# A two-layer streaming encoder: forget gate in quarter tiles, queries' norm weights applied after the turn back, last outputs turned by channel, two splits and four waits moved

## The chip, the cores and the metric

The kernel runs on one core of a Trainium2 chip. The core has five engines with instruction streams of their own: TensorE (PE), VectorE (DVE), ScalarE (ACT), GpSimd (POOL) and SyncE (SP, which only issues DMAs here). They meet through semaphores. The metric is the device time of one launch in microseconds (us), the median of several runs.

## The reference

One step of an encoder with two layers, on 256 new frames behind 16 meta tokens and 32 frames of a running stream, 304 columns in all (`T`); the model's width is 2048.

```python
# layer 0: mLSTM, 8 heads of 512, INNER = 4096
xm, z = split(rmsnorm(x, norm_g) @ w_in)           # 2048 -> 2 x 4096
xc = silu(causal_conv(xm, buf, conv_w, conv_b))
q, k = einsum(xc, wq), einsum(xc, wk) * 512 ** -0.5   # per head
v = einsum(xm, wv)
ig, lf = gates of (q, k, v) @ w_gate                # lf = log_sigmoid
h, (C, n, m) = mlstm_run(q, k, v, ig, lf, state)    # decayed scores, old state C0 enters with a * (q @ C0)
y = ((layernorm(h) * out_g + skip * xc) * silu(z)) @ w_out;  x = x + y
# shared keys, values and forget stream
kvf = rmsnorm(x, kv_norm_g) @ w_kvf                 # 2048 -> 2048 + 2048 + 16
k = rmsnorm(kvf[..., :2048] by head, k_norm_g);  v = kvf[..., 2048:4096]
logf = log_sigmoid(kvf[..., 4096:] + b_f)           # the forget gate, 16 heads
# layer 1: attention with forgetting, 16 heads of 128
q, z = split(rmsnorm(x, norm_g) @ w_in);  q = rmsnorm(q by head, q_norm_g)
s = q @ k.T * 128 ** -0.5 + cumsum(logf)[query] - cumsum(logf)[key], causal
x = x + ((softmax(s) @ v) * silu(z)) @ w_out
```

Returned are the outputs of both streams and all keys, values, forget values and states.

## The kernel before

**Chunks.** Every large weight comes in chunks of 512 rows by 256 columns, 400 in all. A chunk goes through four steps, each on its own engine and each with four buffers: SP loads it (`load_chunk`, `raw`, L146), ACT rounds it to `w_hi` (`high_part`, L152), DVE makes the rest `w_lo` (`low_part`, L157), and PE multiplies (`products`, L177 to L179): for two output tiles `m` and four row tiles `k` it adds w_hi·x_hi, w_hi·x_lo and w_lo·x_hi, 24 matmuls in fp32r, into the PSUM tiles `acc`. SP loads chunk n once DVE has split chunk n - 4; ACT and DVE split n + 2 while they belong to chunk n.

**Slots.** The order of every engine is written by hand: one loop over chunks, and beside each chunk small events with a letter. All engines walk through the same tables (`FIRST_NEXT`, `BESIDE_OUT`, `END_OUT`, `BESIDE`), each with its own function for a letter; an event that comes early in a slot delays the split behind it on ACT and DVE. In the tables of the first layer `O` is PE's outputs of a head, and for ACT and DVE the split of the old sums (`high_old`, `low_old`); `D` are the denominators' sums. In the second layer `q` turns the queries to tokens, `r` and `n` make their norms, `f` the final queries, `b` turns them back, `X` are scores, `y` the outputs' turn.

**Stages.** x is turned to channels and scaled beside the first eight chunks (`START`, `BESIDE0`); then come the eight heads' projections, 14 chunks each (`turn`, with the score products and transposes of the head before in `post`); the last head's turn (`last_z`, `last_qkv`) also makes the gates; then eight rounds of recurrence beside the z and out projections (`state_turns`); 64 chunks of keys and values (`kv_*`, four groups of 16), of which the first group also has the norm (`norm_1`, `columns`) and the forget gate (`extras` on PE, `forget_1` to `forget_3`); and 96 chunks of the second layer (`fox_*`).

**The forget gate before.** `wf` is 128 columns wide per row tile: 16 columns w_hi, at 32 another 16 w_lo, the rest zero. Per row tile two matmuls, against x_hi and x_lo, 32 in all, fill `aux[3]`; DVE adds the two strips, scales with rstd and adds the bias.

**The queries before.** `q_finals` multiplies each of 12 pieces of 128x128 by its norm (a column) and by `gq`, the norm weights repeated on all partitions by one DMA; PE then turns the pieces back (`q_back`) and DVE copies them out of PSUM.

**The end.** `turn_y(c)` turns four channel tiles of x to three PSUM banks, one per block of tokens, once all four tiles have been summed; ACT and DVE copy the banks out, SP stores them.

## Time and profile before

| | us |
|---|---|
| median of 3 runs (lowest, highest) | 1683.02 (1681.72, 1683.88) |
| the profiled execution: time, span | 1681.52, 1679.7 |
| PE busy, PE weight loads busy | 1655.9, 1587.4 |
| DVE, ACT, POOL busy | 1075.7, 804.8, 301.8 |
| HBM read, written | 260.5 MB, 46.8 MB |

The span is the time in which the engines work; launch and end lie outside. The granted clock of PE was 1.00 over the span. The page cuts the span in 40 slices of 42 us: PE is at 9 tenths in all but the first and the last, DVE between 4 and 8, ACT between 3 and 5. PE's busy time is that of modelled ends, so the start times of its matmuls are the safer measure.

### The profile page before, as it was taken

To read this page: it belongs to the slowest core of one execution; us is meant where nothing else is said; L and a number is where in the kernel's file an instruction comes from. 1 tells how busy PE (TensorE), PEld (TensorE's weight loads), DVE (VectorE), ACT (ScalarE), POOL (GpSimd) and SP (SyncE) were. 2 spreads that over 40 slices of the span, in tenths; PEclk is the share of its full clock that TensorE was granted. 3 is DMA by queue.
4 is the path that set the end of the run, shared out by engine and by line. 5 is a ranking of instruction groups with operands and counts; after the bars stand their busy time and mean duration, and the time that the engine had idled before them with its cause. 6 is when DMAs were issued, how large, how long until landed. Compare 5 with 4: busy or idle time off the path is not lost.

```text
span 1679.7 us, 29485 instructions
## 1 busy us (share of the span) xinstructions
PE 1655.9 (99%) x11873; PEld 1587.4 (95%) x11873; DVE 1075.7 (64%) x2074; ACT 804.8 (48%) x1339; POOL 301.8 (18%) x580
## 2 busy tenths in 40 slices
PE   8999999999999999999999999999999999999998
PEld 6999999999988999999999989999999998999998
DVE  5966655655558868768687788665535645563755
ACT  5545344544554534445344445554443555535443
POOL 1202220122143332222322222021112000000000
PEclk9999999999999999999999999999999999999999
DMA  6546554655586676666766655365558554555533
GB/s 189 168 138 218 168 181 137 207 179 179 154 264 187 204 240 183 224 190 199 240 183 224 190 180 176 114 217 187 184 190 285 179 163 150 168 182 164 155 113 108
DMA packets 244344, 309.26 MB, mean 184 GB/s; under 512 B 14056, under 2 KB 219648, under 8 KB 244208
## 3 DMA queue, kind: packets, MB, share of 16 engines
q1 hardware_dynamic: 214352, 215.32, 42.1%
q0 software_dynamic: 29200, 91.23, 15.7%
q8 instruction: 94, 1.54, 0.4%
q10 hardware_dynamic: 656, 0.82, 0.2%
q14 instruction: 42, 0.34, 0.1%
HBM read 260.53 MB, written 46.79 MB: 183 GB/s over the span
## 4 chain that ended last, share of the span: by engine, by line
PE 88%; DVE 6%; ACT 3%; issue 1%; DMA 1%; ACTq 0%; POOL 0%; DVEq 0%
PE acc L177 24%; PE acc L178 24%; PE acc L179 24%; PE aux L1460 3%; PE aux L1302 2%; DVE w_lo L157 2%; PE aux L1433 1%; PE aux L1307 1%; ACT w_hi L152 1%; PE aux L1280 1%; PE aux L2710 1%; PE aux L1467 1%; PE aux L1479 1%; PE aux L2117 1%; DVE q_t L2523 1%
## 5 line engine op out<-in xcount | busy, mean ns | idle before, releaser
L157 DVE TENSOR_TENSOR w_lo<-raw,w_hi 128x1024 fp32r<-128x1024 f32 x400 | 485.7, 1221 | 371.6 <-ACT w_hi L152 369.9
L177 PE MATMUL acc<-xg_hi,w_hi 128*128 128x304 f32 x1536 | 472.8, 308 | 2.9 <-issue 1.6
L152 ACT ACTIVATE w_hi<-raw 128x1024 fp32r<-128x1024 f32 x400 | 413.9, 1055 | 104.8 <-PE acc L179 78.5
L179 PE MATMUL acc<-xg_hi,w_lo 128*128 128x304 f32 x1536 | 463.9, 302 | 0.0
L178 PE MATMUL acc<-xg_lo,w_hi 128*128 128x304 f32 x1536 | 463.0, 301 | 0.0
L177 PEld LDWEIGHTS acc<-xg_hi,w_hi 128*128 128x128 f32 x1536 | 289.6, 189 | 5.7 <-issue 1.8
L178 PEld LDWEIGHTS acc<-xg_lo,w_hi 128*128 128x128 f32 x1536 | 290.5, 189 | 0.9
L179 PEld LDWEIGHTS acc<-xg_hi,w_lo 128*128 128x128 f32 x1536 | 289.8, 189 | 0.0
L104 POOL TENSOR_TENSOR cell<-cell 1x1 f32<-1x1 f32 x159 | 73.7, 463 | 1107.8 <-DVE xc_lo L875 320.1
L177 PE MATMUL acc<-xb_hi,w_hi 128*128 128x288 f32 x512 | 156.3, 305 | 0.9 <-DVE w_lo L157 0.9
L177 PE MATMUL acc<-hz_hi,w_hi 128*128 128x304 f32 x512 | 155.3, 303 | 0.4 <-DVE zs L938 0.4
L178 PE MATMUL acc<-hz_lo,w_hi 128*128 128x304 f32 x512 | 155.1, 303 | 0.0
L179 PE MATMUL acc<-hz_hi,w_lo 128*128 128x304 f32 x512 | 154.3, 301 | 0.0
L179 PE MATMUL acc<-xb_hi,w_lo 128*128 128x288 f32 x512 | 151.9, 297 | 0.0
L178 PE MATMUL acc<-xb_lo,w_hi 128*128 128x288 f32 x512 | 151.7, 296 | 0.0
L177 PEld LDWEIGHTS acc<-xb_hi,w_hi 128*128 128x128 f32 x512 | 96.6, 189 | 2.0 <-DVE w_lo L157 1.6
L177 PEld LDWEIGHTS acc<-hz_hi,w_hi 128*128 128x128 f32 x512 | 96.4, 188 | 1.2 <-DVE hz_lo L1188 0.8
L178 PEld LDWEIGHTS acc<-xb_lo,w_hi 128*128 128x128 f32 x512 | 96.5, 188 | 0.4
L179 PEld LDWEIGHTS acc<-hz_hi,w_lo 128*128 128x128 f32 x512 | 96.7, 189 | 0.0
L178 PEld LDWEIGHTS acc<-hz_lo,w_hi 128*128 128x128 f32 x512 | 96.2, 188 | 0.3
L179 PEld LDWEIGHTS acc<-xb_hi,w_lo 128*128 128x128 f32 x512 | 96.1, 188 | 0.0
L730 ACT ACTIVATE C_out<-aux 128x512 f32<-128x512 f32 x32 | 19.2, 599 | 131.7 <-PE aux L1460 130.0
(499 smaller groups left out, 3000.9 us busy)
## 6 DMA issues: line engine op xcount, KB each, us to landing
raw<-in_a_w_in SPq DMA_DIRECT2D x128, 512.0 KB, 4.0
raw<-in_a_w_out SPq DMA_DIRECT2D x64, 512.0 KB, 4.3
raw<-in_w_kvf SPq DMA_DIRECT2D x64, 512.0 KB, 4.8
raw<-in_b_w_in SPq DMA_DIRECT2D x64, 512.0 KB, 4.6
raw<-in_b_w_out SPq DMA_DIRECT2D x32, 512.0 KB, 3.5
raw<-in_a_wq SPq DMA_DIRECT2D x16, 512.0 KB, 3.8
raw<-in_a_wk SPq DMA_DIRECT2D x16, 512.0 KB, 3.6
raw<-in_a_wv SPq DMA_DIRECT2D x16, 512.0 KB, 5.0
```

What stands on the lines that cost most here:

```text
L104: own.done(own.eng.tensor_tensor(cell, cell, cell, ALU.mult))
L152: act.activation(w_hi[:, s, :, :], raw[:, s, :, :], ACT.Copy).then_inc(hi_made, 1)
L157: dve.tensor_tensor(w_lo[:, s, :, :], raw[:, s, :, :], w_hi[:, s, :, :].bitcast(F32), ALU.subtract).then_inc(lo_made, 1)
L177: pe.matmul(acc[b][:, 0:width], wh, x_hi[:, k0 + k, :], start=st, stop=False)
L178: pe.matmul(acc[b][:, 0:width], wh, x_lo[:, k0 + k, :], start=False, stop=False)
L179: mm = pe.matmul(acc[b][:, 0:width], wl, x_hi[:, k0 + k, :], start=False, stop=last and k == 3)
L730: act.activation(C_out[:, d % 2, :], aux[u.turn(3)][:, :], ACT.Copy).then_inc(b_free[u.turn(3)], 1)
L1280: mm = pe.matmul(gate_sum[r:r + 32, 0:T], wg_in[:, HT * g + d, :], (q_T, k_T, v_T)[g][:, d, :], start=h.a == 0 and g == 0, stop=h.a == LAS ...
L1302: mm = pe.matmul(aux[b][0:n, c:c + T - t0], k_T[:, d, t0:t0 + n], q_T[:, d, t0:T], start=d == 0, stop=d == HT - 1)
L1307: mm = pe.transpose(aux[b][0:n, d * P:(d + 1) * P], (k_T, v_T)[(k - 2) // 3][:, d, t0:t0 + n], ident[:, :])
L1433: mm = pe.matmul(aux[b][:, :], p_, v_, start=k == 0, stop=t < 2 and k == len(parts) - 1)
L1460: mm = pe.matmul(aux[b][:, :], k_, v_, start=k == 0, stop=k == len(parts) - 1)
```

## The change

Eight edits:

1. `START`: ACT splits chunk 0 before it scales x columns 0 to 3; DVE splits it after column 0 and not after column 1; PE goes through chunk 0 by `k` and not by `m`. The squares of x (`squares`) go from chunks 2, 3, 3 to chunks 0, 2, 3.
2. `tokens_taken` of the last head's turn stands ahead of chunk 1 and not of chunk 0.
3. `take_pairs` is cut in two: after the last head the first copy stands ahead of `gates_whole`, the others behind it.
4. Letter `L` takes over the split of the old sums; for head 0 it stands one slot before `O` and ahead of `D`. Elsewhere it stands where `O` did. `set_old_fold` moves to `E`.
5. Forget gate: `wf` becomes 32 columns of fp32, scaled by `kv_norm_g` on DVE; 16 matmuls against x itself go to four quarter tiles (32 columns of PE each, `tile_position`), and one more matmul with `f_fold` adds the four quarters. The steps around it move by one or more chunks.
6. Queries: `q_finals` multiplies by the norm alone, three instructions of 128x512; the norm weights are a column per head (`gq`, 128x4, four DMAs) and come in when `q_back` copies out of PSUM.
7. `selections` leave `q_terms` for a slot of their own, `s`.
8. `turn_y` goes by channel tile and writes the three banks in turn; each tile's sum is waited for by itself.

```diff
-        def products(pe, n, tile, x_hi, x_lo, k0, first, last, ready=None):
+        def products(pe, n, tile, x_hi, x_lo, k0, first, last, ready=None, by_k=False):
...
+            steps = [(m, k) for k in range(4) for m in range(2)] if by_k else [(m, k) for m in range(2) for k in range(4)]
...
-        FIRST_NEXT = {0: "E P Q", 1: "D", 2: "O Z", 3: "N M", 4: "K", 5: "T0 T1", 6: "T2 T3 S0 S1 H0 H1",
+        FIRST_NEXT = {0: "E P Q", 1: "L D", 2: "O Z", 3: "N M", 4: "K", 5: "T0 T1", 6: "T2 T3 S0 S1 H0 H1",
...
+            high_part(act, Count(0))
             act.wait_ge(par_taken, 1)
-            high_x(range(0, 2))
-            high_part(act, Count(0))
-            high_x(range(2, 4))
+            high_x(range(0, 4))
             high_part(act, Count(1))
...
-                for t in {2: (0,), 3: (1, 2)}.get(n, ()):
+                for t in {0: (0,), 2: (1,), 3: (2,)}.get(n, ()):
                     squares(t)
...
-            parts_of(range(0, 2))
+            take_x(0)
+            take_x(1)
+            low_x(0)
             low_part(dve, Count(0))
+            low_x(1)
             parts_of(range(2, 4))
...
                 if j == 4:
+                    take_pairs(Count(LAST))
                     gates_whole()
-                    take_pairs(Count(LAST))
+                    take_more_pairs(Count(LAST))
...
-                if j == 0:
+
+                if j == 1:
                     tokens_taken(Count(LAST - 1))
...
-        wf = sb("wf", [P, KD, P], F32R, p3)
+
+        wf = sb("wf", [P, KD, 32], F32, p3)
+        f_all, f_fold = sb("f_all", [P, T], F32, p3), sb("f_fold", [P, BH], F32, p3)
...
+            def forget_0():
+                dve.wait_ge(f_done, 1)
+                dve.tensor_copy(f_all[:, :], aux[3][:, 0:T]).then_inc(f_out, 1)
...
-                if j == 9:
+                if j == 10:
                     pe.wait_ge(cols_taken, 1)
-                    pe.wait_ge(f_lo, 1)
+                    pe.wait_ge(f_scaled, 1)
+
                     for k in range(KD):
-                        for part, x in enumerate((xk_hi, xk_lo)):
-                            mm = pe.matmul(aux[3][:, 0:T], wf[:, k, :], x[:, k, :], start=k == 0 and part == 0,
-                                           stop=k == KD - 1 and part == 1)
+                        r = 32 * (k % 4)
+                        mm = pe.matmul(aux[3][r:r + 32, 0:T], wf[:, k, :], xT[:, k, :], start=k < 4, stop=k >= KD - 4,
+                                       skip_group_check=True, tile_position=(0, r))
                     mm.then_inc(f_done, 1)
                 if j == 11:
+                    pe.wait_ge(f_out, 1)
+                    pe.matmul(aux[3][0:BH, 0:T], f_fold[:, :], f_all[:, :], start=True, stop=True).then_inc(f_done, 1)
+                if j == 12:
                     pe.wait_ge(f_dve, 1)
...
-        QUERIES = {0: "q", 1: "r n K0 K1", 2: "f K2 K3", 4: "b"}
...
+        QUERIES = {0: "q", 1: "r n K0 K1", 2: "f K2 K3", 3: "s", 4: "b"}
...
-                pool.dma_start(gq[:, :], src.unsqueeze(0).to_broadcast([P, HD])).then_inc(gq_landed, 16)
+                for m in range(GRP):
+                    pool.dma_start(gq[:, m:m + 1], src[m * P:(m + 1) * P].rearrange("(p a) -> p a", a=1))\
+                        .then_inc(gq_landed, 16)
...
-                dve.wait_ge(gq_landed, 16 * (g + 1))
                 for t in range(3):
-                    for m in range(GRP):
-                        d = slice(m * P, (m + 1) * P)
-                        k = GRP * t + m
-                        ins = dve.scalar_tensor_tensor(q_t[:, t, d], q_t[:, t, d], qst[:, 3, k:k + 1], gq[:, d],
-                                                       ALU.mult, ALU.mult)
-                    ins.then_inc(q_final, 1)
+                    y = qst[:, 3, GRP * t:GRP * (t + 1)].unsqueeze(2).to_broadcast([P, GRP, P])
+                    dve.tensor_tensor(head_parts(q_t[:, t, :], P), head_parts(q_t[:, t, :], P), y, ALU.mult)\
+                       .then_inc(q_final, 1)
 
             def q_back(g):
+
+                dve.wait_ge(gq_landed, 16 * GRP * (g + 1))
...
-                for u in range(tile, tile + 4):
+                banks = [free_bank(use(LAST_G, f"y{c}", t)) for t in range(3)]
+                for k in range(4):
+                    u = tile + k
                     pe.wait_ge(acc_free[u % 4], u // 4 + 1)
-                for t, (t0, _) in enumerate(QT):
-                    bank = free_bank(use(LAST_G, f"y{c}", t))
-                    for k in range(4):
+                    for bank, (t0, _) in zip(banks, QT):
                         mm = pe.transpose(bank[:, k * P:(k + 1) * P], xT[:, 4 * c + k, META + t0:META + t0 + P],
                                           ident[:, :])
```

How the instructions stand. ACT beside the first chunks, before, from the first scaling on: `xg_hi` are scaled x columns, `w_hi` splits of a chunk, `sq_junk` squares of x.

```order
L580 ACTIVATE xg_hi<-xT,par 128x304 x2
L152 ACTIVATE w_hi<-raw 128x1024
L580 ACTIVATE xg_hi<-xT,par 128x304 x2
L152 ACTIVATE w_hi<-raw 128x1024
L580 ACTIVATE xg_hi<-xT,par 128x304 x2
L152 ACTIVATE w_hi<-raw 128x1024
L580 ACTIVATE xg_hi<-xT,par 128x304 x3
L152 ACTIVATE w_hi<-raw 128x1024 x2
L580 ACTIVATE xg_hi<-xT,par 128x304 x3
L590 ACTIVATE sq_junk,small<-x_tok 128x2048
```

The same stretch now:

```order
L152 ACTIVATE w_hi<-raw 128x1024
L580 ACTIVATE xg_hi<-xT,par 128x304 x4
L152 ACTIVATE w_hi<-raw 128x1024
L580 ACTIVATE xg_hi<-xT,par 128x304 x2
L152 ACTIVATE w_hi<-raw 128x1024
L590 ACTIVATE sq_junk,small<-x_tok 128x2048
L580 ACTIVATE xg_hi<-xT,par 128x304 x3
L152 ACTIVATE w_hi<-raw 128x1024 x2
L580 ACTIVATE xg_hi<-xT,par 128x304 x3
L590 ACTIVATE sq_junk,small<-x_tok 128x2048
```

The first split has passed two scalings, and the first squares five more and two splits.

DVE at head 0, before, from the end of the denominators' sums (`aq_sum`) to the split of the old sums (`old_lo`); `fold` is the matrix that adds their four strips.

```order
L1096 TENSOR_TENSOR Dm<-Dm,aq_sum 128x48
L1099 MEMSET fold 128x128
L1102 CAST fold<-ident 32x32 x4
L157 TENSOR_TENSOR w_lo<-raw,w_hi 128x1024
L1107 TENSOR_TENSOR old_lo<-aux,old_hi 128x512
```

Now, from the pairs' rest to the start of the sums:

```order
L1084 TENSOR_TENSOR P_hi<-Dm,P_hi 32x96
L157 TENSOR_TENSOR w_lo<-raw,w_hi 128x1024
L1114 TENSOR_TENSOR old_lo<-aux,old_hi 128x512
L1093 TENSOR_TENSOR Dm<-Dm 128x176
L1094 TENSOR_SCALAR aq_sum<-aq,n 128x48
```

`old_lo` has passed the whole of the sums, the fold's setup and one chunk's split.

DVE in the first group of keys, before, from the columns of the norm (`rcol`) on: `f_` are the forget gate's rows, `kst` the keys' norms.

```order
L2043 COPY rcol<-aux 128x1 x3
L157 TENSOR_TENSOR w_lo<-raw,w_hi 128x1024
L2050 COPY f_low<-aux 16x304
L2051 TENSOR_TENSOR f_sum<-f_low,aux 16x304
L2052 TENSOR_TENSOR f_sum<-f_sum,rstd_row 16x304
L2053 TENSOR_SCALAR f_f<-f_sum,bf 16x304
L2054 SCALAR_TENSOR_TENSOR f_abs<-f_f 16x304
L157 TENSOR_TENSOR w_lo<-raw,w_hi 128x1024
L1968 TENSOR_REDUCE kst<-k_sq 128x4 x2
```

Now:

```order
L2052 COPY rcol<-aux 128x1 x3
L157 TENSOR_TENSOR w_lo<-raw,w_hi 128x1024
L2063 COPY f_all<-aux 128x304
L157 TENSOR_TENSOR w_lo<-raw,w_hi 128x1024
L1975 TENSOR_REDUCE kst<-k_sq 128x4 x2
L1975 TENSOR_REDUCE kst<-k_sq 48x4
L1978 TENSOR_SCALAR kst<-kst 128x12
L2069 TENSOR_TENSOR f_sum<-aux,rstd_row 16x304
L2070 TENSOR_SCALAR f_f<-f_sum,bf 16x304
L2071 SCALAR_TENSOR_TENSOR f_abs<-f_f 16x304
```

The rows of the forget gate stand one split and the keys' sums later, and a copy of all four quarters (`f_all`) stands where they were.

## Rows read from the trace of the kernel before

**Rows 1.** The page, part 1: busy us (share of the span) and instructions of each engine.

```profile
PE 1655.9 (99%) x11873; PEld 1587.4 (95%) x11873; DVE 1075.7 (64%) x2074; ACT 804.8 (48%) x1339; POOL 301.8 (18%) x580
```

**Rows 2.** PE's waits: engine line <- who it waited for: us, times, longest.

```profile
PE acc L177 <- issue: 2.6, 4, 1.6
PE acc L177 <- DVE w_lo L157: 2.2, 4, 0.8
```

**Rows 3.** Timeline, PE near 45: start, length, engine, line [idle before <- releaser].

```profile
42.74 0.41 PE L177 MATMUL acc<-xg_hi,w_hi 128*128 128x304 f32 x1 [0.80 <-DVE w_lo L157]
...
47.38 1.06 PE L1361 MATMUL aux<-diag,ones 128*128 128x128 f32 x6 [0.28 <-DVE diag L824]
48.51 0.41 PE L177 MATMUL acc<-xg_hi,w_hi 128*128 128x304 f32 x1
```

**Rows 4.** First chunk: its load, its landing (DMA issues, us to landing), the splits.

```profile
2.13 0.99 SPq L146 DMA_DIRECT2D raw<-in_a_w_in  x2
...
raw<-in_a_w_in SPq DMA_DIRECT2D x1, 512.0 KB, 6.0
...
9.99 1.23 DVE L157 TENSOR_TENSOR w_lo<-raw,w_hi 128x1024 fp32r<-128x1024 f32 x1 [0.41 <-ACT w_hi L152]
...
40.38 1.04 ACT L152 ACTIVATE w_hi<-raw 128x1024 fp32r<-128x1024 f32 x1
```

**Rows 5.** Timeline, PE at the last head's turn.

```profile
431.80 3.97 PE L1302 MATMUL aux<-q_T,k_T 128*128 128x304 f32 x24 [1.03 <-ACT v_T L549]
```

**Rows 6.** Timeline, DVE and PE near 480.

```profile
479.75 0.47 DVE L986 COPY gate_all<-aux 128x304 f32<-128x304 f32 x1 [0.32 <-PE aux L1280]
...
480.66 1.09 PE L1307 MATMUL aux<-ident,k_T 128*128 128x128 f32 x8 [0.98 <-DVE S_st L882]
```

**Rows 7.** Timeline, DVE and PE at head 0.

```profile
515.18 0.68 DVE L1107 TENSOR_TENSOR old_lo<-aux,old_hi 128x512 fp32r<-128x512 f32 x1
...
515.92 0.50 PE L1437 MATMUL aux<-old_hi,fold 128*128 128x512 f32 x1 [1.61 <-DVE old_lo L1107]
...
532.61 0.53 DVE L1181 SCALAR_TENSOR_TENSOR skip_in<-aux,par,skip_in 128x304 f32<-128x304 f32 x1
```

**Rows 8.** PE: gates, their fold, and the forget gate (line L2167: ns, first and last start).

```profile
112.40 0.72 PE L1280 MATMUL aux<-q_T,wg_in 128*32 128x304 f32 x8
...
114.07 3.51 PE L1302 MATMUL aux<-q_T,k_T 128*128 128x304 f32 x16
...
485.02 0.72 PE L1288 MATMUL aux<-gate_all,gate_fold 128*64 128x304 f32 x2
...
1067.90 1.54 PE L2159 MATMUL aux<-ident,rstd_row 128*128 128x1 f32 x12 [0.70 <-DVE ntmp L2036]
...
L2167 PE MATMUL aux<-xg_hi,wf x16: 297/302/305, 1072.7 to 1076.9; 128*128 128x304 f32 x16
...
1086.34 0.60 PE L2174 MATMUL aux<-ident,clf 128*16 128x128 f32 x4 [1.01 <-DVE f_abs L2054]
```

**Rows 9.** Key norm and queries on DVE and PE; tile gq: us to landing.

```profile
1096.27 1.89 DVE L1979 TENSOR_TENSOR k_t<-k_t,kst 128x512 f32<-128x512 f32 x3
...
1391.36 3.24 DVE L2523 SCALAR_TENSOR_TENSOR q_t<-q_t,qst,gq 128x128 f32<-128x128 f32 x12
...
1395.79 0.40 PE L177 MATMUL acc<-xb_hi,w_hi 128*128 128x288 f32 x1 [0.48 <-DVE w_lo L157]
...
1459.98 0.42 DVE L2511 CAST sel<-minus 128x512 fp32r<-128x512 f32 x1
...
1462.00 0.37 PE L177 MATMUL acc<-oz_hi,w_hi 128*128 128x288 f32 x1 [0.40 <-issue]
...
DMA to landing us min/median/max: 4.8/5.8/6.7
```

**Rows 10.** Timeline, PE and SP at the end.

```profile
1674.94 1.50 PE L2783 MATMUL aux<-ident,xT 128*128 128x128 f32 x12 [1.11 <-DVE xT L2598]
...
1677.14 0.45 SPq L2315 DMA_DIRECT2D out_y_sample<-y_tok  x1
```

More of the change, by code:

```diff
@@ L158, in low_part @@
                               ALU.subtract).then_inc(lo_made, 1)
-        def products(pe, n, tile, x_hi, x_lo, k0, first, last, ready=None):
+        def products(pe, n, tile, x_hi, x_lo, k0, first, last, ready=None, by_k=False):
             s = n.turn(SLOTS)
             wait(pe, lo_made, n + 1)
-            for m in range(2):
+            steps = [(m, k) for k in range(4) for m in range(2)] if by_k else [(m, k) for m in range(2) for k in range(4)]
+            width = x_hi.shape[-1]
+            for m, k in steps:
                 u = tile + m
                 b = u.turn(4)
-                width = x_hi.shape[-1]
-                if first:
+                if first and k == 0:
                     wait(pe, acc_free[b], u.rounds(4))
-                for k in range(4):
-                    if ready and not m:
-                        ready(k)
-                    wh = w_hi[:, s, k, m * P:(m + 1) * P]
-                    wl = w_lo[:, s, k, m * P:(m + 1) * P]
-                    st = first and k == 0
-                    pe.matmul(acc[b][:, 0:width], wh, x_hi[:, k0 + k, :], start=st, stop=False)
-                    pe.matmul(acc[b][:, 0:width], wh, x_lo[:, k0 + k, :], start=False, stop=False)
-                    mm = pe.matmul(acc[b][:, 0:width], wl, x_hi[:, k0 + k, :], start=False,
-                                   stop=last and k == 3)
+                if ready and not m:
+                    ready(k)
+                wh = w_hi[:, s, k, m * P:(m + 1) * P]
+                wl = w_lo[:, s, k, m * P:(m + 1) * P]
+                st = first and k == 0
+                pe.matmul(acc[b][:, 0:width], wh, x_hi[:, k0 + k, :], start=st, stop=False)
+                pe.matmul(acc[b][:, 0:width], wh, x_lo[:, k0 + k, :], start=False, stop=False)
+                mm = pe.matmul(acc[b][:, 0:width], wl, x_hi[:, k0 + k, :], start=False,
+                               stop=last and k == 3)
             mm.then_inc(used, 1)
@@ L1903, in turn @@
                         high_xb(j)
-                    if first and j == 6:
-                        high_wf()
                     if first and j == 7:
                         inverse_rms()
-                    if first and j == 11:
-                        forget_2()
                     if j in (3, 7):
@@ L1921, in turn @@
                         inverse_norms(g)
+                    if first and j == 12:
+                        forget_2()
             counted["values out"] = values_by_token
@@ L2011, in turn @@
                     if first and j == 10:
-                        forget_1()
-                    if first and j == 12:
-                        forget_2()
+                        forget_0()
                     if j == 11:
                         norm_terms(g)
-                    if first and j == 15:
+                    if first and j == 11:
+                        forget_1()
+                    if g.a == 1 and j == 0:
                         forget_3()
@@ L2020, in turn @@
                         keys_final(g)
+                    if first and j == 14:
+                        forget_2()
                     if j == 15:
@@ L2354, in fox_gpsimd @@
                 kc_load(g)
-                pool.wait_ge(q_final, 3 * g)
+                for t in range(3):
+                    freed(pool, use(g - 1, "b", t))
                 settled(own, cell[:, :])
@@ L2607, in event @@
                     q_terms(g)
+                elif e == "s":
+                    selections(g)
                 elif e == "f":
```

89 lines of the change are left out of this document (48 added, 41 removed).

## Prediction

> **What bounds the kernel now.** I read the page's busy times first. TensorE (PE) is busy for 1655.9 of 1679.7 us [rows 1], so the kernel can get shorter in two ways only: less work on PE, or less of the 23.8 us in which PE stands. Then I listed who PE waited for. No wait is long, and the engines named change: w_lo (VectorE, DVE) four times for 2.2 us, and "issue" four times for 2.6 us, where the profile names nobody [rows 2]. So I went through PE's timeline from end to end and took each stall by its place. A stall costs a little more than the idle time printed: matmuls overlap, and about 0.1 us of restart is hidden in each. I therefore compare the start of the matmul after the stall with the start that it would have without one. In steady work one matmul with 304 columns follows the last after 0.14 us (16 of them, every second one, from 1072.7 to 1076.9 [rows 8]), so a chunk of 24 takes 3.34 us.
>
> The span is 1679.7, the profiled execution 1681.5, the median of the three runs 1683.0. I work out a difference on the trace and take it from the median.
>
> **The start.** Two edits. Firstly, ScalarE (ACT) now splits the first weights before it scales x columns 0 and 1. These weights are issued at 2.13 and land 6.0 later, at 8.1 [rows 4]. The split takes 1.04 [rows 4], so w_hi is there at 9.2, against 9.95 before. But DVE now makes x_lo of column 0 between, and that waits for ACT's scaling, which has moved behind the split: ACT 9.2 to 9.7, DVE 9.7 to 10.2, and w_lo starts at 10.2 where it started at 9.99 [rows 4]. PE starts 0.2 later. The order by k then lets PE run six matmuls on each column, which hides the later columns; before, they were hardly late. Bounds: w_lo can't start before the weights have landed and been split (0.8 sooner), and a slower hand-over costs 0.4. I take +0.2, the value by the rows.
>
> Second, the squares of x move: one of the three (about 2 us on ACT) from chunk 3 to chunk 0, where ACT only waited for columns. At chunk 3 they ended just ahead of the split at 40.38 [rows 4], for which DVE and then PE waited: 0.80 at 42.74; its x columns and the norm's diagonals came late for the same reason, 0.28 at 47.38 [rows 3]. ACT is 2.0 sooner, PE wanted 0.8. From 41.94 to 48.51 are 6.57; without stalls it is one chunk, 3.34, and 1.13 for the small matmuls (47.38 to 48.51 [rows 3]): 2.1 less. The diagonals are then just in time: -2.0. If the last of x lands later than ACT's idle time, the squares delay columns 6 and 7 by 0.3. Start in all -1.8 (-2.9 to -1.0).
>
> **The last head's turn.** The wait for all four accumulators moves from before the score products to one chunk later. PE waited 1.03 at 431.80 for ACT's copy of v_T, which these products don't read [rows 5]: with the restart -1.1. One chunk later that copy is long done. Next, one pair copy now precedes gates_whole on DVE. PE waited 0.98 at 480.66 for that copy, which stood behind gate_all at 479.75 [rows 6]. DVE was busy until 479.4 (0.32 before gate_all [rows 6]), so PE's first transposes start at 479.85; but the next bank is freed by the copies that stay behind gate_all, at 480.85. The chunk starts at 481.3 instead of 481.5: -0.2 only.
>
> **Head 0's old sums.** PE stood for 1.61 at 515.92 until DVE had made old_lo at 515.18 to 515.86 [rows 7]: a chunk's split, the sums and the fold's setup lay ahead of it. Now old_lo comes right after that chunk's split, at about 511.2 to 511.9, the sums end at 513.7, and PE, which gets there at 514.2, waits for neither. The fold's setup (1.0 us) moves to where DVE waited 1.1 for ACT's exponentials. PE gains 1.75. But DVE itself gains only 1.0 (the norm waits for the next split, which ACT does after the silu), and at 532.61 to 533.14 it frees the bank that PE takes for the second state [rows 7], with 0.3 of slack. PE stands again there for 0.45: -1.25 (-1.75 if DVE keeps up, -0.9 if not).
>
> **The forget gate.** Before: 32 full matmuls, 32 x 0.139 = 4.44. After: 16 fp32 matmuls in quarter tiles and one fold. The gate products of the first layer have the same form: twelve of them, four after four, took 1.67, from 112.40 to the score products at 114.07, with the way back to full tiles [rows 8]. Sixteen make 2.2. The fold has its like at 485.02, 0.72 [rows 8]. So 2.95, 1.5 less. The bound on the bad side: if four quarters didn't run beside one another, each would take what a full fp32 product of this width does (two passes of twice 0.14, some 0.5), 16 x 0.5 = 8.1.
>
> The Trainium skill (TensorEngine Tiling (Array Packing), Key Properties) says that a change of the tiling mode drains the engine. That speaks against the edit, which adds four changes. It puts no price on one. Three rounds of four beside one another would be 1.5, and the trace has 1.67 for them, so a switch in and out can't cost more than about 0.2; a drain of that size is in my 2.2 and 0.72, and by the rule with a dearer one, say 0.5 each, the forget gate would save 1.2 less.
>
> Two stalls go as well: 0.70 at 1067.90, since the columns of the norm are now asked for one chunk later, and 1.01 at 1086.34, where the cache's transposes waited for forget_1 [rows 8]; with restarts 1.9. What is late next? I followed DVE and ACT to the end of this group with durations of the trace. The copy of f_all is done 2.8 before the fold wants it; forget_1 1.8 before the transposes; the last key copy 0.8 before the keys' transposes; w_lo of the second chunk of the next group 0.6 before its products, since forget_2 (2.8 us) now stands right before it. Each is covered, the last two barely; should they slip, 1 to 1.5 come back. Forget gate -3.4 (-3.6 to -1.9).
>
> **The queries' norm weights.** Twelve multiplications of 128x128, 3.24 in all at 1391.36, become three of 128x512 with a broadcast; that form took 1.89 for three in the key norm [rows 9]. DVE is 1.35 sooner, ahead of the split on which PE waited: chunk at 1395.79 after 0.48, with two waits inside the transposes before it [rows 9]. There PE is bound by DVE still: w_lo 1.35 sooner, -1.3. The same place in the other three groups: 1321.84 (0.41), 1470.18 (0.24, an accumulator freed late), 1568.58 (0.46): -0.6, -0.45, -0.65. The selections, 0.5 us [rows 9], leave the slot in which PE waited 0.40 for an accumulator at 1462.00 and 0.39 at 1560.18: -0.5 and -0.45. In their new slot DVE has the 1.35 to pay for them. The gain now comes in when the turned queries are copied out of PSUM: a multiplication of that size from PSUM took 0.68 [rows 7], some hundredths over a copy, and PE has 1 us left there. Queries -3.95 (-4.4 to -2.2).
>
> The weights' load becomes four DMAs of 4-byte elements: 1.7 us more on POOL's queue, ahead of kT_in and the values. Both have tens of us.
>
> **The end.** All 12 transposes waited for the last sum: 1674.94 after 1.11 [rows 10]. Now nine can be done by then, and the three banks fill 0.3 sooner, 0.4 for the first copy and 0.9 for the last. But SyncE issues three stores in a row, of which the last begins at 1677.14 and lasts 0.45 [rows 10], and it can start them only 0.35 sooner: -0.35 (0 to -0.65). The three earlier turns have no stall: nothing.
>
> **The sum.** -1.8 -1.1 -0.2 -1.25 -3.4 -3.95 -0.35 = -12.05. I give 0.4 back for the two near ties: -11.65, so 1671.4. With all terms at their good ends -14.5 (1668.5), with all at their bad ends -6.7 (1676.3).
>
> **The rivals.**
> 1. DVE and ACT become the bound. In each place PE is only 0.3 to 2 us ahead of DVE, and the profile already shows one such chain (head 0). If half of the gain is given back within the same stage, the time is 1677.2. Against it: in the long runs of chunks between these places DVE is busy 64% and catches up. 15%.
> 2. The quarter tiles run one after another: +5.9 on the forget gate, 1677.3. The trace's 0.54 for four speaks against it. 2%.
> 3. Transfers bound the chunks: PE comes earlier and finds weights that haven't landed. that ACT waits for raw in several turns speaks for it; that no stall of PE goes back to one speaks against it, and each load is issued by the split four chunks before, which moves along. Then only PE's saved work stays: 1681.5. 5%.
> 4. Slower: the weights for the queries come late. Each group's four loads are 512 packets of 4 bytes, and DVE waits for them in q_back with the next splits queued behind it. The old load landed in 4.8 to 6.7 us [rows 9]. For group 0, issue to use is 38 us; only beyond that does PE wait, and it takes 50 us to eat the gain: 1684 and more from there. 2%.
> That the edit in the first chunk is worth nothing is in the sum.
>
> **How the numbers follow.** Forecast 76%, rivals 15, 2, 5, 2. What can be told from no change is 0.2%, 3.4 us. Below 1679.6 lie the forecast and rivals 1 and 2: faster 0.92; rival 3 and mishaps that add up: same 0.05; rival 4: slower 0.03. The range runs from 1668.3 to 1677.3, where the first two rivals end.
>
> **What would show it.** PE's stalls at 42, 47, 431, 515, 1067, 1086, 1321, 1393 to 1395, 1462, 1470, 1560 and 1568 are gone; one of about 0.4 appears near 530 and one of 0.4 stays near 480; the first product starts at 11.5. Sixteen quarter matmuls take 2.2. The last three stores start 0.35 after one another's time of before. The prediction is wrong if w_lo or k_final is named for over 1 us near 1090, or if PE stands under 3 us less than before.

## The result, and the profile after

| | before | after |
|---|---|---|
| median, us (lowest to highest) | 1682.86 (1681.72 to 1683.88, 4 runs) | 1670.26 (1668.49 to 1670.61, 4 runs) |
| ratio, 95% interval | | 0.9922 (0.991 to 0.9934) |
| profiled execution: time, span | 1681.52, 1679.7 | 1668.49, 1666.7 |
| PE idle in the span | 23.8 | 15.7 |

12.6 us less, where 11.65 were forecast. One execution of before, run once more later on, took 3274.33 us with a granted clock of 1.00 beside one of 1682.8; it stands in none of the comparisons, and no trace of it is there to say why. The page's first part of the changed kernel, beside [rows 1]:

```profile
PE 1651.0 (99%) x11875; PEld 1582.7 (95%) x11875; DVE 1068.1 (64%) x2041; ACT 803.4 (48%) x1338; POOL 306.8 (18%) x592
```

PE works 4.9 us less and stands 8.1 less. Whom it still waits for (us, times, longest), beside [rows 2]:

```profile
PE aux L1345 <- DMA x_tok<-in_x_sample: 3.1, 1, 3.1
PE aux L1351 <- DMA rows<-in_a_norm_g: 2.7, 1, 2.7
PE acc L177 <- DVE w_lo L157: 2.5, 2, 2.3
PE aux L1469 <- DVE skip_in L1188: 0.6, 1, 0.6
PE aux L2738 <- DVE q_new L2563: 0.5, 1, 0.5
PE acc L177 <- DVE zs L943: 0.4, 1, 0.4
PE aux L1314 <- DVE S_st L886: 0.4, 1, 0.4
PE aux L1442 <- issue: 0.3, 1, 0.3
```

8.2 of the 15.7 now lie in the first 12 us, before the first product can start (the first three waits). To see where the rest went I laid the two timelines of PE side by side and took the difference of the starts at each landmark. Those of the changed kernel that answer to [rows 3, 5 to 10], PE unless the row says DVE or SPq:

```profile
12.03 0.59 PE L177 MATMUL acc<-xg_hi,w_hi 128*128 128x304 f32 x1 [2.34 <-DVE w_lo L157]
...
24.24 0.41 PE L177 MATMUL acc<-xg_hi,w_hi 128*128 128x304 f32 x1 [0.23 <-DVE xg_lo L803]
...
45.54 1.06 PE L1369 MATMUL aux<-diag,ones 128*128 128x128 f32 x6
46.67 0.41 PE L177 MATMUL acc<-xg_hi,w_hi 128*128 128x304 f32 x1
...
428.75 3.89 PE L1309 MATMUL aux<-q_T,k_T 128*128 128x304 f32 x24
...
477.49 0.66 PE L1314 MATMUL aux<-ident,k_T 128*128 128x128 f32 x4 [0.36 <-DVE S_st L886]
...
507.63 0.68 DVE L1114 TENSOR_TENSOR old_lo<-aux,old_hi 128x512 fp32r<-128x512 f32 x1
...
510.59 0.40 PE L1446 MATMUL aux<-old_hi,fold 128*128 128x512 f32 x1
...
1071.15 2.25 PE L2187 MATMUL aux<-xT,wf 128*32 128x304 f32 x32
1073.34 0.41 PE L177 MATMUL acc<-xg_hi,w_hi 128*128 128x304 f32 x1
...
1076.88 0.69 PE L2192 MATMUL aux<-f_all,f_fold 128*16 128x304 f32 x2
...
1384.80 0.41 PE L177 MATMUL acc<-xb_hi,w_hi 128*128 128x288 f32 x1 [0.18 <-DVE w_lo L157]
...
1388.73 0.30 PE L2738 MATMUL aux<-F,sel 128*128 128x144 f32 x1 [0.47 <-DVE q_new L2563]
...
1664.00 0.44 SPq L2339 DMA_DIRECT2D out_y_sample<-y_tok  x1
```

The chunk behind the diagonals starts at 46.67 and started at 48.51 [rows 3]; the last head's scores at 428.75, no stall, for 431.80 [rows 5]; head 0's fold at 510.59, no stall, for 515.92 [rows 7], 2.3 us after `old_lo` is done. One row is new: the second group's first scores wait 0.47 for `q_new`. The differences by part:

| part | forecast | between the two profiles |
|---|---|---|
| start | -1.8 | -1.84 |
| last head's scores | -1.1 | -1.21 |
| its transposes | -0.2 | -0.56 |
| head 0 | -1.25 | -1.34 (1.72, less 0.38 behind it) |
| rest of the heads | 0 | -0.33 |
| forget gate | -3.4 | -3.48 |
| queries | -3.95 | -3.90 (4.37, less the 0.47 at 1388) |
| end | -0.35 | -0.35 |
| given back for near ties | +0.4 | 0 |
| sum | -11.65 | -13.0 |

The 0.33 in the rest of the heads is scatter: it lies at the last head's fold of the old sums near 983, where PE's starts are 0.54 apart in the profile of before and under 0.3 in that of the changed kernel, but 0.57 and 0.61 in two later profiles of kernels with the same code there. One profile of each is one sample; the experiments say which of these numbers hold.

### The profile page after: what moved, and what is told of

Its sections match the earlier page's. It is cut to its first block, busy times and chain, and to the rows that moved or that the text cites. A ratio compares the mean times of both kernels' runs of the same rounds, so it can differ in the third digit from the quotient of the medians.

```text
span 1666.7 us, 29469 instructions
## 1 busy us (share of the span) xinstructions
PE 1651.0 (99%) x11875; PEld 1582.7 (95%) x11875; DVE 1068.1 (64%) x2041; ACT 803.4 (48%) x1338; POOL 306.8 (18%) x592
## 3 DMA queue, kind: packets, MB, share of 16 engines
q8 instruction: 94, 1.54, 0.4%
## 4 chain that ended last, share of the span: by engine, by line
PE 94%; DVE 2%; ACT 1%; DMA 1%; SPq 0%; issue 0%; ACTq 0%; DVEq 0%
PE acc L177 26%; PE acc L178 25%; PE acc L179 25%; PE aux L1469 3%; PE aux L1309 2%; PE aux L1442 2%; PE aux L1314 1%; PE aux L1287 1%; PE aux L2740 1%; DMA x_tok<-in_x_prompt 1%; PE aux L1476 1%; PE aux L2134 1%; PE aux L1488 1%; PE aux L2797 0%; DVE w_lo L157 0%
```

## The experiments

The theory: each part gives what its PE work and its stalls were worth, and they add up. Four kernels undo one part each; the end, with -0.35, got no experiment of its own. The landmarks are the first matmuls of the 400 chunks: I take the difference of their starts in two profiles, and a part's worth is how much that difference changes across it.

**Forget gate undone.**

```diff
-wf = sb("wf", [P, KD, 32], F32, p3)
+wf = sb("wf", [P, KD, P], F32R, p3)
-        mm = pe.matmul(aux[3][r:r + 32, 0:T], wf[:, k, :], xT[:, k, :], ..., tile_position=(0, r))
+        for part, x in enumerate((xk_hi, xk_lo)):
+            mm = pe.matmul(aux[3][:, 0:T], wf[:, k, :], x[:, k, :], ...)
-    if j == 9:   # columns of the norm
+    if j == 8:
```

> The changed kernel with the forget gate as before: 32 full matmuls of 304 columns on split data, the columns of the norm asked for at chunk 8, the cache's transposes behind forget_1. Theory (the sum of the prediction): +3.4 us over the changed kernel, that is about 1673.7; 1.5 of it are matmuls (0.139 each, 4.44 against 2.25 + 0.69), 1.9 two stalls of PE of 0.70 and 1.01 with their restarts, which come back behind the norm's diagonal products and ahead of the cache's transposes. Rival 'DVE and ACT are the bound': the key norm sets the end of this group, the chunk behind it doesn't come later than the work on PE makes it, so +1.5 or less. Rival 'the quarter tiles cost what they save': +1.9 (the stalls alone).

Measured: 1674.24 (1672.79 to 1675.2), ratio to before 0.9936 (0.9922 to 0.9949). PE's starts are 0.44 later than in the changed kernel ahead of the part and 5.50 behind it: 5.06, more than expected. The windows (PE, PEld, DVE, ACT, POOL busy, then PE's granted clock, DMA share, GB/s) and the timeline behind the stall that came back show why:

```profile
1065.00:1066.00 1.00, 1.00 (x9) 1.00 (x9) 0.65 (x7) 0.00 (x0) 0.00 (x0) 0.93 0.45 76
1066.00:1067.00 1.00, 1.00 (x6) 1.00 (x6) 0.00 (x0) 0.00 (x0) 0.00 (x0) 0.50 0.94 334
1067.00:1068.00 1.00, 1.00 (x5) 1.00 (x5) 0.00 (x0) 0.00 (x0) 0.00 (x0) 0.50 1.00 321
1068.00:1069.00 1.00, 1.00 (x5) 1.00 (x5) 0.00 (x0) 0.00 (x0) 0.00 (x0) 0.50 0.83 281
1069.00:1070.00 1.00, 1.00 (x8) 1.00 (x8) 0.00 (x0) 0.00 (x0) 0.00 (x0) 0.86 0.11 38
```

```profile
1063.05 1.54 PE L2168 MATMUL aux<-ident,rstd_row 128*128 128x1 f32 x12 [0.70 <-DVE ntmp L2045]
1064.46 0.38 PE L177 MATMUL acc<-xg_hi,w_hi 128*128 128x304 f32 x1
...
1069.42 0.30 PE L2176 MATMUL aux<-xg_hi,wf 128*128 128x304 f32 x1
```

The same chunk in the kernel before, at a granted clock of 1.00:

```profile
1069.30 0.39 PE L177 MATMUL acc<-xg_hi,w_hi 128*128 128x304 f32 x1
...
1072.72 0.30 PE L2167 MATMUL aux<-xg_hi,wf 128*128 128x304 f32 x1
```

The granted clock went to 0.50, 1.2 GHz, from 1066 to 1069, behind a stall of 0.70 and twelve matmuls of one column. The chunk took 4.96 (1064.46 to 1069.42) for 3.42 before: 1.54 lost. What is left, 3.5, is the part itself, as forecast and as between the two profiles. I hadn't thought of the clock at all.

**Queries undone.**

```diff
-    y = qst[:, 3, GRP * t:GRP * (t + 1)].unsqueeze(2).to_broadcast([P, GRP, P])
-    dve.tensor_tensor(head_parts(q_t[:, t, :], P), head_parts(q_t[:, t, :], P), y, ALU.mult)
+    for m in range(GRP):
+        ins = dve.scalar_tensor_tensor(q_t[:, t, d], q_t[:, t, d], qst[:, 3, k:k + 1], gq[:, d], ...)
-QUERIES = {0: "q", 1: "r n K0 K1", 2: "f K2 K3", 3: "s", 4: "b"}
+QUERIES = {0: "q", 1: "r n K0 K1", 2: "f K2 K3", 4: "b"}     # selections in "r"
```

> The changed kernel with the queries' norm as before: twelve multiplications of 128x128 with the norm and its weight, the selections ahead of them in the slot of the squares' sums, one load of the weights. Theory: +3.95 by the prediction's terms, less 0.5 for a stall that the trace of the changed kernel shows anew (0.47 ahead of the second group's first scores, behind the selections on DVE) and that goes here: +3.5, about 1673.8. PE's stalls of 0.4 to 0.5 come back in all four groups behind the transposes of the queries, and in the third and fourth at the chunk behind the sums. Rival 'the engines beside PE take the time back': under +2, since PE comes later to the scores and finds them ready.

Measured: 1673.55 (1672.64 to 1674.35), ratio 0.9933 (0.9921 to 0.9945). The landmarks move by 3.68, from +2.23 ahead of the queries to +5.91 behind them, where 3.5 were expected; 0.2 of it lies at the first group's scores, where no term had anything. The rival is out.

**Three edits of the heads undone.**

```diff
-FIRST_NEXT = {0: "E P Q", 1: "L D", ...
+FIRST_NEXT = {0: "E P Q", 1: "D", ...      # old sums in "O", fold's setup behind "D"
-if j == 1: tokens_taken(Count(LAST - 1))
+if j == 0: tokens_taken(Count(LAST - 1))
-take_pairs(Count(LAST)); gates_whole()
+gates_whole(); take_pairs(Count(LAST))
```

> The changed kernel with three edits of the heads undone: the wait for the last head's accumulators one chunk earlier, both copies of the pairs behind gate_all, and head 0's old sums behind the sums with the fold's setup between. Theory: 1.1 + 0.2 + 1.25 = +2.55 by the prediction's terms; by the starts read from the trace of the changed kernel the three gave 1.2 + 0.5 + 1.4 = +3.1. So +2.5 to +3.2, about 1673. Rival 'DVE is the bound behind head 0': its part is under 0.9, since PE then stands at the second state instead: +2.2 or less. In the profile: a stall of 1.6 at head 0's fold, one of 1.0 at the last head's scores, one of 1.0 at the last head's transposes.

Measured: 1673.38 (1672.36 to 1676.86), ratio 0.9935 (0.9923 to 0.9948). The profile is of the slowest execution, 1676.86, and shows the clock again. The heads' scores are 1.19 later and the transposes 0.55, close to the two profiles' 1.21 and 0.56. At head 0 the stall is back (1.78 at the fold), and behind it the clock falls; windows as above:

```profile
514.00:516.00 2.00, 0.62 (x3) 0.19 (x1) 1.94 (x4) 1.98 (x3) 0.00 (x0) 1.00 0.53 179
516.00:518.00 2.00, 1.77 (x9) 1.69 (x10) 1.30 (x2) 0.52 (x1) 0.00 (x0) 0.74 0.60 189
518.00:520.00 2.00, 2.00 (x9) 2.00 (x10) 1.88 (x8) 0.00 (x0) 0.00 (x0) 0.50 0.66 207
520.00:522.00 2.00, 2.00 (x10) 2.00 (x10) 1.59 (x10) 0.47 (x2) 0.00 (x0) 0.50 0.39 133
522.00:524.00 2.00, 2.00 (x10) 2.00 (x10) 1.83 (x7) 2.00 (x4) 0.00 (x0) 0.55 0.00 0
```

By the transposes of `hn` another 3.19 are lost. Head 0's own part is 1.78, less the 0.47 that VectorE takes back behind it: 1.3, so the rival (under 0.9) is out. The other four executions kept a mean clock of 1.000, with spans of 1670.5 to 1672.3.

**Start undone.**

```diff
-high_part(act, Count(0)); act.wait_ge(par_taken, 1); high_x(range(0, 4))
+act.wait_ge(par_taken, 1); high_x(range(0, 2)); high_part(act, Count(0)); high_x(range(2, 4))
-for t in {0: (0,), 2: (1,), 3: (2,)}.get(n, ()):
+for t in {2: (0,), 3: (1, 2)}.get(n, ()):
# and back as well: VectorE's order around the first split, by_k=False
```

> The changed kernel with the start as before: the first weights split behind two scaled columns, the first chunk by output tile and not by column, and all three squares late (one at chunk 2, two at chunk 3). Theory: +1.8, about 1672.1: two stalls come back at the fourth and fifth chunk (0.8 ahead of a chunk, 0.3 ahead of the norm's diagonals), together 2.0, and the first products start 0.2 to 0.7 sooner. Rival 'the early split and the order by column give something too': in the trace of the changed kernel the small transposes behind the first chunk came 0.46 sooner although the first product came 0.71 later; then +2.3 or more. Rival 'the landing of x and of the weights decides': the difference is within +-0.6, and lies in landings, not in stalls for w_lo.

Measured: 1671.53 (1671.25 to 1671.61), ratio 0.9921 (0.9907 to 0.9934). The chunk behind the diagonals starts at 48.05, 1.38 later than in the changed kernel's first profile, with both old stalls back (0.78, 0.30). The rest of this run's excess lies at head 0, where PE waited 1.35 for "issue" and not 0.29. Before this chunk the landings of x and the weights differ from run to run, so I took the start of that chunk over all profiles: 48.51, 48.25, 48.17, 48.05 with the old start; 46.67, 46.36, 47.25, 48.10, 46.99, 47.18, 47.37, 48.38, 46.39 with the new one, mean 48.24 and 47.19. The start gives 1.06, not 1.84. How much of it the early split and the order by column give, and how much the squares, was not taken apart.

One source of that spread can be read from the traces. In the changed kernel's first profile the products of the first chunk change their pace (no line is left out between the first two nor between the last two):

```profile
13.43 0.46 PE L179 MATMUL acc<-xg_hi,w_lo 128*128 128x304 f32 x1
13.69 0.46 PE L177 MATMUL acc<-xg_hi,w_hi 128*128 128x304 f32 x1
...
15.11 0.30 PE L177 MATMUL acc<-xg_hi,w_hi 128*128 128x304 f32 x1
15.25 0.30 PE L178 MATMUL acc<-xg_lo,w_hi 128*128 128x304 f32 x1
```

They start 0.253 apart and then 0.139. 0.253 is also their distance in the stretch at half the clock of the first experiment (1066 to 1069). The windows print 1.00 here, but the trace's list of granted clocks has nothing ahead of 14.96 in this profile, and a time without an entry is printed as full clock. Its first entry, 1.0, begins at 14.5 to 18.6 us over the fourteen profiles, and in each of them the last slow distance of the first chunk ends within 0.2 of it. So PE runs the first 3 to 6 us of the products at the pace of 1.2 GHz, and the 1.00 of a span or of an execution says nothing of them. The first profile of before got the full clock at 16.85 and that of the changed kernel at 14.96, which is part of the 1.84; over the four and the nine profiles the means are 15.97 and 15.96, so the 1.06 is free of it.

**The kernel before again, for its clock.** No edit.

> The kernel before once more, for its clock. In the runs of before timed beside the last four kernels the mean granted clock was 1.000 in two (spans 1680.3 and 1680.6) and 0.998 in seven (1682.0 to 1684.2). Clock theory: in some executions the granted clock falls to 0.5 (1.2 GHz) for some us behind a stall that the change takes away: behind head 0's fold (as in the kernel with the heads' edits undone, where it cost 3.2 us from 516 to 524) or behind the norm's columns near 1070 (as with the forget gate undone, 1.6 us). Then this profile either shows a span near 1680 and no such stretch, or 1682 to 1684 and one there. Rival: the drop lies anywhere, also where nothing was changed.

Measured: span 1681.0, mean clock 0.999, and the stretch is where the theory put it:

```profile
514.00:516.00 2.00, 0.39 (x3) 0.01 (x1) 1.97 (x4) 1.98 (x3) 0.00 (x0) 1.00 0.33 114
516.00:518.00 2.00, 2.00 (x12) 1.91 (x13) 1.61 (x6) 0.29 (x1) 0.00 (x0) 0.85 0.69 217
518.00:520.00 2.00, 2.00 (x10) 2.00 (x9) 1.97 (x5) 0.00 (x0) 0.00 (x0) 0.50 0.68 208
520.00:522.00 2.00, 2.00 (x14) 2.00 (x13) 1.49 (x12) 1.10 (x3) 0.00 (x0) 0.80 0.29 103
```

It cost 1.54. The stall for `old_lo` was 1.61 in all three profiles that have it at head 0; what differed was the idle time for "issue" some 6 us ahead of it: 0.24 with no fall, 0.60 and 0.95 with one. A wait for "issue" of 1.35 to 1.67 without the stall behind it (three profiles) made none.

**The kernel before with head 0's edit alone.**

```diff
-FIRST_NEXT = {0: "E P Q", 1: "D", ...
+FIRST_NEXT = {0: "E P Q", 1: "L D", ...    # and the fold's setup from "D" to "E"
```

> The kernel before with one edit of the change: head 0's old sums ahead of the denominators' sums, the fold's setup beside the exponentials. Step of the prediction: -1.25 (-0.9 to -1.75) in executions in which the clock stays at 1.0: spans of 1678.6 to 1679.3 against 1680.4. Clock theory: the stall of 1.6 behind which the clock fell is gone, so executions with a mean clock of 0.998 become rare, and the median falls by up to 3 more: about 1681 against 1684.9. Rival: the clock falls elsewhere; then the share of executions at 0.998 stays and the median moves by 1.25 alone.

Measured: 1681.38 (1678.63 to 1682.38, 11 runs), before 1682.98 (15 runs), ratio 0.9988 (0.9979 to 0.9997). PE's starts: 1.78 sooner at the fold, 1.39 behind the states. The 0.4 comes back inside the first state, whose last two matmuls took 1.02 and 0.63 before:

```profile
513.98 0.39 PE L1437 MATMUL aux<-old_hi,fold 128*128 128x512 f32 x1
...
531.27 1.02 PE L1460 MATMUL aux<-vt,kt 96*128 96x512 f32 x2
```

Five of eleven executions still had a mean clock of 0.999, against 11 of 15 of before beside them at 0.999 or 0.998; the two shares alone don't prove a difference. So this stall is one source of falls and not the only one; the norm's columns in the first experiment are another.

**Two moves on VectorE.**

```diff
-take_pairs(Count(LAST)); gates_whole(); take_more_pairs(Count(LAST))
+take_pairs(Count(LAST)); take_more_pairs(Count(LAST)); gates_whole()
-QUERIES = {0: "q", 1: "r n K0 K1", 2: "f K2 K3", 3: "s", 4: "b"}
+QUERIES = {0: "q", 1: "r s n K0 K1", 2: "f K2 K3", 4: "b"}    # first two groups
```

> The changed kernel with two moves on VectorE: both copies of the last head's pairs ahead of gate_all (it waits 1.1 there for the gates), and the queries' selections of the first two groups right behind the squares' sums, where it waits 2.2 for the next split. Theory, by the stalls that the trace of the changed kernel names at these places: the 0.36 ahead of the last four transposes near 477.5 goes (-0.45 with the restart), the 0.47 ahead of the second group's first scores goes (-0.5), nothing comes instead: -0.95, about 1669.3 with a span of 1665.8. Rival: gate_all is late by the second pair of copies and PE waits for the gates' fold instead (first part 0), and q_new is not held up by the selections but by the transposes (second part 0): no change.

Measured: 1668.81 (1667.31 to 1669.3), ratio 0.9917 (0.9903 to 0.9931). Both stalls are gone, and the landmarks behind them come 0.59 (from +0.35 to -0.24) and 0.47 sooner. Expected were 0.45 and 0.5.

**All quarters in one quarter.**

```diff
-r = 32 * (k % 4)
+r = 0        # and the fold reads one quarter
```

> The changed kernel with all sixteen quarter matmuls of the forget gate in the same quarter of the array, so that none can run beside another; the fold then reads one quarter. If the four quarters of the changed kernel run side by side (the prediction): 16 full fp32 matmuls of 304 columns in a row. The key norm's sum of squares, two such in 0.67, says some 0.28 at least and with its gaps up to 0.56 each, so 4.5 to 9 in place of 2.25: +2.3 to +6.7. If they run one after another anyway (the prediction's second rival, or a dear mode change that sets the 2.25): no change within 0.3.

Measured: 1675.66 (1675.12 to 1676.27), ratio 0.9959 (0.9947 to 0.9972). PE's line, where the changed kernel has 2.25 at 1071.15:

```profile
1071.87 8.38 PE L2187 MATMUL aux<-xT,wf 128*32 128x304 f32 x32
```

8.38 / 16 = 0.52 for one alone, 0.14 for each of four side by side. The second rival is dead, and its price was near (8.1): the starts behind are 6.13 later, where it had 5.9.

**The changed kernel again.** No edit.

> The changed kernel again, beside before, for the clock of their executions and for the start. Clock theory: of 24 timed executions of before whose clock is known 18 had a mean granted clock of 0.999 or 0.998 and took some 2 to 3 us longer than those at 1.000; of the changed kernel and of those with both clock-prone stalls gone it was 2 of 22. So this one is at 1.000 in at least four of five, with spans of 1666 to 1669, and the gain between executions at 1.000 is 11.5 to 12.5, between medians up to 3 more. Rival: the clock has nothing to do with the change: the share at 0.999 and below is as large as before's. Start: the first product at 11.5 to 12.1, the chunk behind the norm's diagonals at 46.4 to 47.3 (before: 48.2 to 48.5), so -1.15 on the average and not -1.8.

Measured: 1669.62 (1668.12 to 1670.45), before beside it 1683.59 (1681.76 to 1686.73), ratio 0.9913 (0.9899 to 0.9928). One of four at 0.999. Over all runs, before was at 0.999 or less in 24 of 31 timed executions, the changed kernel in 2 of 8, neither below 0.999. At a mean clock of 1.000 the spans are 1678.8 to 1680.6 (mean 1679.8 of 8, the first profile among them) and 1666.3 to 1668.8 (mean 1667.8 of 6).

**A better version.** The two moves above, and in the start:

```diff
-low_x(0); low_part(dve, Count(0)); low_x(1)
+low_part(dve, Count(0)); low_x(0); low_x(1)
+if n == 2: squares(0)        # ahead of high_x
-for t in {0: (0,), 2: (1,), 3: (2,)}.get(n, ()):
+for t in {2: (1,), 3: (2,)}.get(n, ()):
```

> The kernel of the last experiment on VectorE (pairs' copies and selections moved) with two more moves in the start. VectorE makes w_lo of the first chunk ahead of x_lo of column 0, as ScalarE's w_hi is there before the scaled column; and the first squares run behind the split at chunk 2 and not at chunk 0, where they waited for the last of x (landing at 21.2 to 22.5 in the traces) and held up columns 6 and 7. Theory: first product at 11.4 to 11.6 (-0.45), no stall near 24 (-0.3 to -0.8), chunk behind the diagonals at about 46.0; with the 0.9 of the last experiment 1668.0 or less against 1670.3. Rival 'the squares only move their delay': columns 9 to 11 come late for the chunk at 33, and a stall comes back there. Rival 'the first products are bound by the landings of x and weights': the first product stays at 11.9 or later.

Measured: 1667.02 (1666.84 to 1668.39), ratio 0.9901 (0.9886 to 0.9916); the changed kernel beside it 1669.62. The first product waits for x_lo of column 0 now, and the chunk behind the diagonals comes at 46.41:

```profile
11.78 0.59 PE L177 MATMUL acc<-xg_hi,w_hi 128*128 128x304 f32 x1 [2.53 <-DVE xg_lo L805]
...
45.28 1.06 PE L1371 MATMUL aux<-diag,ones 128*128 128x128 f32 x6
46.41 0.41 PE L177 MATMUL acc<-xg_hi,w_hi 128*128 128x304 f32 x1
```

Between them no stall over 0.2 is named, so the squares' new place is free in this profile. Expected were 11.4 to 11.6 and 46.0: ScalarE's first split began 0.15 later in this run than in the changed kernel's profile, and the full clock came at 16.1 and not at 15.0. One profile can't show what the start's two moves give, as 46.41 lies within the spread of the nine (46.36 to 48.38). The spans at a mean clock of 1.000 are 1665.0 to 1666.6 (mean 1665.5 of 4), 2.3 below the changed kernel's 1667.8; the two moves on VectorE account for 1.1 of it.

**Full matmuls between the quarters.** This kernel is for timing only: with the extra matmuls, which start groups of their own in the bank in which the quarters add up, the forget gate's sums come out different.

```diff
+if k in (3, 7, 11):
+    pe.matmul(aux[3][:, 320:448], ident[:, :], xT[:, k, 0:P], start=True, stop=True, ...)
```

> The changed kernel with a full 128x128 fp32 matmul (a transpose into an unused part of the bank) behind each of the first three rounds of four quarter matmuls, so that the array changes its tiling six times more. What it leaves in that part of the bank is read by nobody. Without a price for a change the three cost 3 x 0.13 = 0.4 (twelve such transposes take 1.47 to 1.51): 2.25 becomes 2.65. With the bound of the prediction, at most 0.2 for a way in and out, 2.65 to 3.25. Rival, the Trainium skill's rule with a dear drain (0.25 a change or more): 2.65 + 1.5 = 4.15 or more.

Measured: 1672.03 (2 runs), ratio 0.9929 (0.9909 to 0.9949). The stretch on PE:

```profile
1072.98 0.72 PE L2187 MATMUL aux<-xT,wf 128*32 128x304 f32 x8
1073.63 0.49 PE L2190 MATMUL aux<-xT,ident 128*128 128x128 f32 x2
1074.05 0.72 PE L2187 MATMUL aux<-xT,wf 128*32 128x304 f32 x8
...
1076.18 0.72 PE L2187 MATMUL aux<-xT,wf 128*32 128x304 f32 x8
1076.83 0.41 PE L177 MATMUL acc<-xg_hi,w_hi 128*128 128x304 f32 x1
```

3.85 from the first quarter to the next chunk, 2.19 in the changed kernel: 0.55 for each full matmul put between. Its work is 0.13, so a way out and back costs 0.42, about 0.2 a change. That is beyond my bound (0.2 for both) and near, though short of, the rival's 0.25. How much of it is the fill of a lone matmul was not measured apart. The Trainium skill's rule (TensorEngine Tiling (Array Packing), Key Properties), that a change of mode drains the engine, is in keeping with this trace, which shows the price of the way and not the drain itself.

**Selections of all groups where they stood.**

```diff
-17: "r", 18: "n", 19: "f", 20: "s", 21: "b"
+17: "r s", 18: "n", 19: "f", 21: "b"
```

> The changed kernel with the selections of all four groups right behind the squares' sums, where they stood before. Step of the prediction (stalls of 0.40 and 0.39 for an accumulator at 1462.00 and 1560.18 of before, behind the selections): they come back in the third and fourth group, +0.95, with the starts 1457.47 and 1554.70 of the changed kernel at about 1457.5 and 1555.7 less what the second group gains; there the 0.47 ahead of the first scores goes, -0.5. Sum +0.45. Rival: with the transposed gain DVE has time enough there as well, and the accumulator is free: -0.5 in all.

Measured: 1669.26 (1668.38 to 1669.88), ratio 0.9913 (0.9896 to 0.9929).

```profile
1450.71 0.37 PE L177 MATMUL acc<-oz_hi,w_hi 128*128 128x288 f32 x1 [0.39 <-issue]
...
1548.42 0.37 PE L177 MATMUL acc<-oz_hi,w_hi 128*128 128x288 f32 x1 [0.39 <-issue]
```

Both stalls are back, 0.48 each by the starts, and the second group gives 0.55: +0.4 by the landmarks, as expected. That is too little for the medians to tell (1669.26, and 1669.62 for the changed kernel beside it). The best table has the selections early in the first two groups and late in the others.

## Why the prediction was right, point by point

**The parts.** They add up, and in each the named stall went. Queries: -3.95, measured 3.90 and 3.68. Their places gave 0.65, 1.35, 0.48, 0.70 for the four groups' waits (forecast 0.6, 1.3, 0.45, 0.65), 0.48 and 0.48 for the selections, and 0.23 that no term had at the first group's scores, less the 0.47 lost in the second. Forget gate: -3.4, measured 3.48 and 3.5; sixteen quarters took 2.19 to 2.25 (forecast 2.2) and the fold 0.69. Neither near tie (k_final, w_lo before forget_2) slipped, and the 0.4 for them wasn't spent. With the start at 1.06 and the end at the 0.35 of the two profiles, the parts of the experiments add up to 11.6 and those of the two profiles, with the start put right and without the 0.33, to 11.9, where the kernels at a mean clock of 1.000 are 12.0 apart.

**Head 0.** -1.25, measured 1.34 and 1.39. The 0.45 that VectorE was to take back near 530 came at 528 (0.38).

**What failed in size.** The start: +0.2 for the first split came out larger. The first product starts at 12.0 on the average (nine profiles of the changed start) and not at 11.5 (four of the old: 11.32 to 11.84), as the weights landed late as well, and the caveat on the last of x came true: it landed at 21.2 in the first profile, the squares ran behind it, and PE waited 0.23 there, up to 1.28 in other profiles. The term had nothing for the clock's late rise either. So the start gives 1.06 and not 1.8, at the bad end of its range. The forecast hit this closely also because its misses offset one another: 0.75 too much for the start; 0.4 for ties that weren't spent, 0.35 at the transposes and 0.23 at the scores too little. The ends of its range are slightly off as sums: the terms' bad ends as written make -7.3 and not -6.7. The transposes: 0.56 and not 0.2; the second bank is free 0.83 after `gate_all` begins (0.47, 0.33 and 0.19, overlapping), and I had put it 1.1 after.

**What failed in kind.** "In their new slot DVE has the 1.35 to pay for them": in the second group it hadn't. PE had gained the same 1.3 there, and q_new, which had been ready 0.26 before the scores, came 0.47 late.

**What I didn't see.** The kernel before loses time to the clock in most executions: its spans average 1679.8 at a mean clock of 1.000, 1681.3 at 0.999 (10 executions) and 1682.8 at 0.998 (13), 1.5 a step, which is what one stretch at half the clock cost in the profiles. The share of executions at 0.999 or less goes with the stalls: 24 of 31 with head 0's stall and that of the norm's columns, 9 of 21 in the three kernels with one of the two, 4 of 36 in the changed kernel and the seven others with neither. The first profile of before has no such stretch, so neither its rows nor my sum had it. A stall alone isn't enough, though: the 0.70 at the norm's columns stands in the first profile of before, too, with no fall behind it. Between executions at 1.000 the gain is 12.0 (forecast 11.65), between medians 12.6 in the first comparison and 14.0 in the last. That the clock is the difference is shown for the two stretches in the profiles at 516 and 1066; for executions without a profile the place of the falls is only argued.

**The rivals.** PE isn't bound by DVE and ACT to the extent of rival 1: 0.38 and 0.47 came back of 13, not half. The quarters run side by side. No stall goes back to a load of weights behind the start. The four small loads of gq landed in 2.8 to 5.7 us, sooner than the one of before [rows 9].

## What to carry to other kernels

Place each stall on TensorE's timeline and price it by the start of the next matmul; the prices add up if you also ask, at every wait that goes, who arrives next and by how much it was early. Where an edit frees both engines at once, work moved into "the time gained" there has no time. Take several profiles before believing the first 50 us or a comparison of a few us, and read the mean clock of every timed execution: a stall can cost more than its idle time.

## What the runs showed of the hardware

- A stall of 1.61 with another 0.60 or 0.95 of idle time some 6 us ahead of it, or one of 0.70 ahead of twelve one-column matmuls, was followed in single executions by 3 to 7 us at half the granted clock, which cost 1.5 to 3.2 us. In the first profile of before both stalls stand with the clock at 1.00 all through.
- At one and the same place, where head 0's values begin, PE stood for "issue" 0.24 to 1.67 us in thirteen of fourteen profiles, whatever the kernel. One pair of profiles can't tell parts of that size.
- A quarter matmul in fp32 of 304 columns takes 0.52 alone and 0.14 beside three others; leaving and entering the quarter tiling costs about 0.2 each, the fill of the lone matmul between included.
- At the start products of 304 columns follow one another after 0.253 us, the pace of a stretch at a granted clock of 0.50, until the trace's first entry of 1.0 (14.5 to 18.6 us into the span), and after 0.139 from there on. The 1.00 printed ahead of that entry stands for no entry.
- With full matmuls put into the free columns of a bank whose quarters still add up (columns 320 to 448, the sums in 0 to 304) those sums changed. That it is their start flag which does it is argued, not shown: no kernel had the matmuls without it.
